# Experts' Silu in one ScalarE function, the attention phase's last jobs in a written-out order, and half of the slot table's one-hots on GpSimd

## The reference, cut to what matters

```
x = x + concat(conv_out, attn_out) @ w_out
h2 = rms_norm(x, norm_ffn_g)
lg, le = h2 @ w_rg, h2 @ w_re            # 4 groups, 32 experts
group = argmax(lg); the two best experts of the group; combine weights
for each block of 128 rows with the same expert e (rows padded per expert):
    y = (silu(xe @ w_g[e]) * (xe @ w_u[e])) @ w_d[e]
    out[token of the row] += y * weight of the row
x = x + out
```

## Time and profile before

| | |
|---|---|
| median of three runs | 2318.94 us |
| the profiled execution, its own time | 2315.55 us |
| its span, first to last instruction | 2313.8 us |
| mean granted TensorE clock | 0.971 |
| PE, DVE, ACT, POOL busy | 93, 73, 57, 33% |

### The profile page before, as it was taken

One profiled execution on the slowest core, in us unless ns is written; L12 is line 12 of the kernel. 1 busy time (PEld: TensorE's weight loads), 2 busy tenths in 40 slices (PEclk: granted clock), 3 DMA queues, 4 the chain that ended last, 5 costly groups with the idle time before them and its releaser, 6 DMA issues. The chain is left out here.

```text
span 2313.8 us, 39978 instructions
## 1 busy us (share of the span) xinstructions
PE 2144.3 (93%) x13278; PEld 1787.7 (77%) x13279; DVE 1687.2 (73%) x2330; ACT 1312.6 (57%) x2435; POOL 755.1 (33%) x678
## 2 busy tenths in 40 slices
PE   8999999994899998899999857999999999999997
PEld 6888888883777886678777745888888888888886
DVE  3798999983676667777888748788688566466644
ACT  5223434334677677766666614678688456465533
POOL 1110565552566554544544501111111111111111
PEclk9999999996999999999999977999999999999999
DMA  6543333325433242332321119999899778768852
GB/s 218 192 157 105 114 124 131 105 100 164 125 94 106 88 132 69 115 116 69 108 79 58 51 73 330 342 311 374 271 374 374 253 215 273 227 220 276 275 173 45
DMA packets 209244, 406.62 MB, mean 176 GB/s; under 512 B 50623, under 2 KB 77119, under 8 KB 209117
## 3 DMA queue, kind: packets, MB, share of 16 engines
q1 hardware_dynamic: 195581, 355.71, 43.8%
q0 software_dynamic: 13536, 49.29, 9.0%
HBM read 312.27 MB, written 92.67 MB: 175 GB/s over the span
## 5 line engine op out<-in xcount | busy, mean ns | idle before, releaser
L2143 DVE TENSOR_TENSOR p_w_lo<-p_raw,p_w_hi 128x1024 fp32r<-128x1024 f32 x384 | 445.9, 1219 | 179.4 <-ACT p_w_hi L1945 175.8
L1790 POOL TENSOR_TENSOR p_wgt<-p_wgt,p_past 128x1024 f32<-128x1024 f32 (+4 forms) x166 | 307.9, 1856 | 354.0 <-DVE p_past L1670 353.8
L1945 ACT ACTIVATE p_w_hi<-p_raw 128x1024 fp32r<-128x1024 f32 x384 | 376.9, 1051 | 62.5 <-PE p_up L2031 51.8
L563 DVE SCALAR_TENSOR_TENSOR p_ut<-p_ut,p_cw 128x512 f32<-128x512 f32 (+1 forms) x480 | 339.5, 782 | 0.0
L1670 DVE TENSOR_TENSOR_SCAN p_past<-p_keep,p_past,p_one 128x513 f32<-128x513 f32 (+1 forms) x196 | 225.9, 1193 | 78.0 <-ACT p_keep L1480 75.4
L298 PE MATMUL p_pj<-p_w_hi,p_xt_hi 128*128 128x512 f32 x680 | 270.9, 398 | 4.2 <-DVE p_xt_lo L539 2.4
L298 PE MATMUL p_pj<-p_w_hi,p_xt_lo 128*128 128x512 f32 x680 | 266.5, 392 | 0.0
L298 PE MATMUL p_pj<-p_w_lo,p_xt_hi 128*128 128x512 f32 x680 | 265.9, 391 | 0.0
L1480 ACT ACTIVATE p_keep<-p_zp 128x512 f32<-128x512 f32 (+3 forms) x326 | 160.2, 547 | 123.1 <-PE p_zp L1351 110.4
L2031 PE MATMUL p_gp<-p_w_lo,p_xt_hi 128*128 128x256 f32 x736 | 206.8, 281 | 0.0
L2031 PE MATMUL p_gp<-p_w_hi,p_xt_lo 128*128 128x256 f32 x736 | 206.7, 281 | 0.0
(11 more groups left out here) (266 smaller groups left out, 4949.0 us busy)
## 6 DMA issues: line engine op xcount, KB each, us to landing
p_raw<-in_w_up SPq DMA_DIRECT2D x128, 512.0 KB
p_raw<-in_w_gate SPq DMA_DIRECT2D x128, 512.0 KB
p_raw<-in_w_down SPq DMA_DIRECT2D x128, 512.0 KB
p_w_raw<-in_w_in SPq DMA_DIRECT2D x40, 256.0 KB, 4.1
p_x<-in_x SPq DMA_DIRECT2D x17, 512.0 KB, 4.3
p_y<-in_x SPq DMA_DIRECT2D x17, 512.0 KB
scr_y<-p_y SPq DMA_DIRECT2D x17, 512.0 KB, 3.0
p_y<-scr_y SPq DMA_DIRECT2D x17, 512.0 KB
```

The costliest lines, as they stand in the source:

```text
L563: dve.scalar_tensor_tensor(dst, src, cw[:, a, j:j + 1], dst, ALU.mult, ALU.add).then_inc(tap_done, 1)
L1790: pool.tensor_tensor(mine, mine, past_rows[:, u % NP, 0:n, 2:2 + w], ALU.mult).then_inc(a_done, 1)
L1945: act.activation(w_hi[:, p, :], raw[:, n % RING, :], ACT.Copy).then_inc(whi_done, 1)
L2143: dve.tensor_tensor(w_lo[:, p, :], raw[:, n % RING, :], w_hi[:, p, :].bitcast(F32), ALU.subtract).then_inc(wlo_done, 1)
```

## The change

In `attention_jobs`, the jobs planned for the steps from the end of the units on are put away, and a list of 14 steps takes their place, with the same jobs. In the tail, `squares` comes in the step of the second `wo` half and `hidden` one step after it (two for the last tile), and DVE's `mean_squares` stands ahead of the jobs. For `o`, ACT squares first and copies second. `rank` no longer uses `le` as scratch.

In `phase_moe`, DVE makes the table of blocks first and then waits for POOL's constants, five instead of six; POOL writes `in_row`. Each half of `gp` gets one Silu by ACT and one multiplication by DVE, without waits of DVE for itself. The second half of transposed `h` gets a place of its own in the unused half of a `gp` bank, PE transposes it before the down projection, and ACT and DVE split it ahead of the next block's rows.

```diff
+    z = 2 * NT - 1
+    tail = [[], [], [("wo", z - 1, 0)], [("h2t", z - 2, 0), ("h2t", z - 2, 1)], [("o", z)],
+            [("wo", z - 1, 1), ("mix", z), ("route", z - 2)], [("wo", z, 0), ("h2t", z - 1, 0), ("h2t", z - 1, 1)],
+            [("wo", z, 1)], [("route", z - 1)], [("h2t", z, 0), ("h2t", z, 1), ("rank", len(BATCHES) - 2)],
+            [("route", z)], [], [], [("rank", len(BATCHES) - 1)]]
...
-        hidden_step = [{m: e + (3 + c if e < len(units) else 2) for m, e in end_step.items() if m >= NT} for c in range(2)]
+        hidden_step = [{m: e + (3 + c if e < end else 1 if m < 2 * NT - 1 else 2)
+                        for m, e in end_step.items() if m >= NT} for c in range(2)]
+        square_step = {m: e + 1 if e < end else e for m, e in end_step.items() if m >= NT}
...
-                    pe.wait_ge(o_sq_done, j[1] + 1)
+                    pe.wait_ge(o_out, j[1] + 1)
...
+                    if i:
+                        act.wait_ge(o_ms, i)
+                    act.activation(o_sq[:, :], rows, ACT.Square).then_inc(o_sq_done, 1)
                     if i >= 2:
                         act.wait_ge(o_done, i - 1)
                     act.activation(o_raw[:, i % 2, :], rows, ACT.Copy).then_inc(o_out, 1)
-                    if i:
-                        act.wait_ge(o_ms, i)
-                    act.activation(o_sq[:, :], rows, ACT.Square).then_inc(o_sq_done, 1)
...
+                elif s - 1 in o_step_of:
+                    mean_squares(o_step_of[s - 1])
...
-        htp = ps("htp", [P, FT, P])
+        htp = ps("htp", [P, 2, P])
+        h_cols = [htp[:, :, :], gp[:, 0, HF:2 * HF].rearrange("p (f t) -> p f t", f=2)]
...
-                act.wait_ge(gs_done[k], b)
-                act.activation(sg[:, bass.ts(k, HF)], gp[:, k, 0:HF], ACT.Sigmoid).then_inc(sg_done[k], 1)
+                act.wait_ge(h_done[k], b)
+                act.activation(sg[:, bass.ts(k, HF)], gp[:, k, 0:HF], ACT.Silu).then_inc(sg_done[k], 1)
...
                 h_hi(b, 0)
+                h_hi(b, 1)
                 x_hi(b + 1)
-                h_hi(b, 1)
...
                     transpose_h(b, 0)
                     transpose_x(b + 1)
+                    transpose_h(b, 1)
                     weights(e, 3)
...
                     half_down(0, 0, True)
-                    transpose_h(b, 1)
                     half_down(1, 0, True)
...
-            dve.wait_ge(consts, 6)
-            link(dve.tensor_copy(iota[:, :], iota_i[:, :]))
...
             dve.sem_inc(table_done, 1)
 
+            dve.wait_ge(consts, 5)
+            link(dve.tensor_copy(iota[:, :], iota_i[:, :]))
...
+            dve.sem_inc(rows_done, 1)
...
-                dve.tensor_scalar(in_row[:, n % RS, :], iota[:, :], row[:, n:n + 1], None, ALU.is_equal)
...
-                dve.tensor_tensor(sg[:, cols], gp[:, k, 0:HF], sg[:, cols], ALU.mult).then_inc(gs_mid[k], 1)
-                dve.wait_ge(gs_mid[k], b + 1)
                 dve.wait_ge(ht_ps[k], b)
                 dve.tensor_tensor(h[:, cols], up[:, cols], sg[:, cols], ALU.mult).then_inc(h_done[k], 1)
-                dve.wait_ge(h_done[k], b + 1)
-                dve.sem_inc(gs_done[k], 1)
...
             def block_of(b, at):
                 rest(at, 0, 1)
-                silu(b, 0)
+                gated(b, 0)
                 rest(at, 1, 2)
+                gated(b, 1)
                 h_rest(b, 0)
-                silu(b, 1)
+                h_rest(b, 1)
                 x_rest(b + 1)
-                h_rest(b, 1)
                 rest(at, 2, PIECES)
...
+            pool.wait_ge(rows_done, 1)
+            for n in range(NC):
+                if n >= RS:
+                    pool.wait_ge(spread, n - RS + 1)
+                pool.tensor_scalar(in_row[:, n % RS, :], iota[:, :], row[:, n:n + 1], None,
+                                   ALU.is_equal).then_inc(row_in, 1)
```

More of the change, by code:

```diff
@@ L903, in attention_jobs @@
         s += 1
+    z = 2 * NT - 1
[3 more added lines that the diff above has]
+            [("route", z)], [], [], [("rank", len(BATCHES) - 1)]]
+    assert sorted(j for x in tail for j in x) == sorted(j for s in placed if s >= end for j in placed[s])
+    placed = {s: js for s, js in placed.items() if s < end} | {end + n: js for n, js in enumerate(tail)}
+    where.update({j: end + n for n, js in enumerate(tail) for j in js})
     return placed, where, first, last, user
@@ L1538, in _ @@
                     decode_mask()
-                for m in at_step(end_step, s - 1):
-                    if m >= NT:
-                        squares(m)
+                for m in at_step(square_step, s):
+                    squares(m)
         @block.vector
@@ L1643, in job @@
                     for k in range(2):
-                        link(dve.tensor_tensor(le[:, 0:hi - lo, :], oh[k][:, 0:hi - lo, :], cand[:, 0:hi - lo, :],
-                                               ALU.mult))
-                        link(dve.tensor_reduce(picks.rank[:, k, lo:hi], le[:, 0:hi - lo, :], AX.X, ALU.add))
+                        mine = oh[k][:, 0:hi - lo, :]
+                        link(dve.tensor_tensor(mine, mine, cand[:, 0:hi - lo, :], ALU.mult))
+                        link(dve.tensor_reduce(picks.rank[:, k, lo:hi], mine, AX.X, ALU.add))
             def piece(n):
@@ L1709, in _ @@
                     second_half(s - 3)
-                if s - 1 in o_step_of:
+                if s < len(units) and s - 1 in o_step_of:
                     mean_squares(o_step_of[s - 1])
@@ L1958, in h_hi @@
                 act.wait_ge(d_done, b)
-                act.activation(ht_hi[:, 2 * k:2 * k + 2, :], htp[:, 2 * k:2 * k + 2, :], ACT.Copy).then_inc(hh_done[k], 1)
+                act.activation(ht_hi[:, 2 * k:2 * k + 2, :], h_cols[k], ACT.Copy).then_inc(hh_done[k], 1)
             def block_of(b, at):
@@ L1964, in block_of @@
                 lead(at, 0, 1)
-                sigmoid(b, 0)
+                gate(b, 0)
                 lead(at, 1, 3)
-                sigmoid(b, 1)
+                gate(b, 1)
                 h_hi(b, 0)
+                h_hi(b, 1)
                 x_hi(b + 1)
-                h_hi(b, 1)
                 lead(at, 3, 6)
@@ L2005, in transpose_h @@
                 pe.wait_ge(h_done[k], b + 1)
-                for f in (2 * k, 2 * k + 1):
-                    last = pe.transpose(htp[:, f, :], h[:, f * P:(f + 1) * P], ident[:, :])
+                for x in range(2):
+                    f = 2 * k + x
+                    last = pe.transpose(h_cols[k][:, x, :], h[:, f * P:(f + 1) * P], ident[:, :])
                 last.then_inc(ht_ps[k], 1)
@@ L2168, in block_of @@
                 rest(at, 0, 1)
[L2169 removed]
+                gated(b, 0)
                 rest(at, 1, 2)
+                gated(b, 1)
                 h_rest(b, 0)
[L2172 removed]
+                h_rest(b, 1)
                 x_rest(b + 1)
[L2174 removed]
                 rest(at, 2, PIECES)
[L2177 removed]
+            for done in (xl_done, *h_done, *hl_done):
                 dve.sem_inc(done, 1)
```

14 lines of the change are left out of this document (7 added, 7 removed).

## The result

The changed kernel takes 2292.8 us (median of four runs, 2290.51 to 2294.42) against 2319.5 us of the kernel before (four runs beside it, 2317.93 to 2320.57): ratio 0.9885, 95% interval 0.9868 to 0.9902. I had forecast 2290 us, range 2279 to 2302. The profiled execution's own time is 2291.98 us, its span 2290.2 us; before they were 2315.55 and 2313.8.

A forecast was written before the change was run, and what follows sets the result against it. A chain through all engines bounds the attention tail, PE the experts' blocks. Terms -15.6 + 0.0 - 4.5 - 8.7 - 0.4 = -29.2 us on 2315.55 give 2286.3, plus the median's 3.4: 2290 us, range 2279 to 2302.

The forecast's parts named there:

- Part 1: Tail of attention: the new order of jobs brings -15.6 us, between -12 and -18.
- half of the 1.8 us that the full clock would give: Tail, Square to router's result: PE idle before this `route` too, so only half the full-clock gain; 15.3 us earlier in all.
- The rival that the picks of batch 3 hold up the last row: Tail: the last row's chain waits for DVE's picks; tail gains only -9 us, 2296 us in all; chance 0.12.
- Part 2: Slot table at the start of the experts' phase: 0.0 us, between -6.1 and +3.
- my 0.55 us a row: Slot table loop: POOL's and DVE's instructions one after the other for the 28 rows not made ahead, 15.4 us.
- the rival, free sharing: Slot table: POOL and DVE don't hold each other up, 6 us more go, 2284 us; chance 0.2.
- the 1.5 us for the block table first: Start of experts' phase: the block table needs no constant, so DVE starts at 1382.3, not 1383.85: -1.5 us.
- Parts 3 and 4: Experts' blocks: 27 intervals without splitting weights gain -4.5 us, 18 with splitting -8.7 us.
- The DMA's rival: Weights' DMA bounds the 12 one-block experts' intervals, staying at 19.26 us; 7.7 us not gained, 2297 us; chance 0.1.
- the splitting blocks' 0.64 us: Blocks with splitting: down projection 0.42 us earlier plus 0.23 us of transposes; -7.7 us over 12 intervals.
- The gain of the first block: First experts' block: adds -0.4 us to the sum.
- the rival of a slower kernel: Experts' blocks: ACT reloads tables at each change between Silu and Copy; 2336 us, or 2349 without the blocks' gain; chance 0.04.

The follow-up runs named there:

- PE kept busy: Kernel with rows shared between POOL and DVE, plus matmuls nobody reads filling PE's idle times: 2282.3 us, ratio 0.9845 to the kernel before.
- Table set once: One single-column Silu by ACT behind the phase's first Exp: 2283.2 us on the changed kernel, 2273.2 us with shared rows and PE kept busy (64 transposes).
- first rows alone: Changed kernel, but DVE stands still until POOL has written its first six one-hot rows: 2295.6 us (single run).

## Why the prediction was right, and where it was not

**Part 1, the tail: right, 1.1 us too much.** Forecast -15.6, measured -14.5. To the end of the last values 6.24 (I took 6.3); then, event by event, `o` came 3.24 us nearer to the values (3.1), `mix` 0.38 to `o` (0.3), the last `wo` 3.61 to `mix` (3.6), the Square 0.95 to `wo` (1.1). The step that failed is the next one, Square to the router's result: I took half of the 1.8 us that the full clock would give, plus 0.3 us for `mean_squares`; the step went from 9.36 to 9.27 us. The `route` stayed at 3.60 us, fully at half clock, and the run with PE kept busy shows what was missing, 7.18 us for this step. The rival that the picks of batch 3 hold up the last row did not come about: DVE's `hidden` started 2.17 us after the Square, at 1353.22, as it had before (2.16). But DVE was busy with picks and copies until that moment, with no time to spare, and nothing in my sum said that it would be just enough: that was luck.

**Part 2, the slot table: the size wrong, +2.6 instead of 0.0.** From DVE's first one-hot to the read it is 19.5 us against 16.5 before, +3.0 where I had +1.1; what lies ahead of that became 0.4 us shorter where I had 1.1. Two terms failed. The first was the price of `in_row` on POOL, 0.29 us from a cast of the same tile, against 0.59 to 0.60 us measured. At 0.59 us, undisturbed, 28 rows are 16.5 us even side by side with DVE (17.2 measured), so the sharing never decided: my 0.55 us a row was near the measured 0.615 for a wrong reason, and the gain of the rival, free sharing, wasn't there to be had. The second was the 1.5 us for the block table first, worth 0.62 alone. The rule of the Trainium skill that I had set beside this (SBUF — State Buffer, "Who interferes with whom") has the right direction: the first row took 1.78 us beside DVE's product of 1088 columns and 0.63 without it. It was not the bound. The range of this part was also added up wrongly: +1.1, +2 and -1.5 make +1.6 at the upper end and not +3, so the measured +2.6 lies outside what my terms allowed.

**Parts 3 and 4, the blocks: right.** Light intervals 18.56 to 18.61 us and once 18.80 (forecast 18.57), one-block 18.57 to 18.62 (18.6), with table loads 20.13 to 20.15 (20.1), in all -13.27 us for -13.2. The DMA's rival is refuted for this kernel: the one-block interval has the same share of 1.05 and 374 GB/s as the earlier trace rows, and still takes 18.57 us. I had put the splitting blocks' 0.64 us down as 0.42 of DVE and 0.23 of the transposes; undone one by one, Silu brings 0.50 and the transposes' place 0.17. The gain of the first block did not show: from the slot table's read to the first `yo` it was 32.38 us before, 32.78 in the changed kernel, and 32.0 to 33.0 in the eight others in which PE wasn't kept busy.

**Table loads.** Eight at the gate's line, as before: Silu and Copy don't drive each other out, and the rival of a slower kernel did not come about. This is what the Trainium skill says of copy (ScalarE: Activation LUTs, "Table sets: the hidden batching unit"), and the trace agrees: 8 loads for 92 Silu. Seven more stand at the line of a Copy (L1958), as before; my prediction did not look at them, and "Table set once" removes them with the eight. I had also taken the gain of parts 3 and 4 off twice in that rival's time: 2289.7 + 59 is 2349 us with the gain, and 2362 without.

**The sum.** The terms give -24.8 us, the profiled executions -23.6, the medians -26.7, against -29.2 forecast: the two misses, tail and slot table, are 3.7 us of the 4.4 between forecast and terms, the first block's 0.8 nearly the rest, and the medians differ by 1.9 us more than the terms, which is within what the unchanged part varies by. So the median's 2292.8 us for 2290 is closer than the terms were: by these it would have been 2294 to 2295. The range's upper end, with part 1 at -12, part 2 at +3 and the DMA's rival, is 2304 us by its own terms and not 2302.

## What to carry to other kernels

Moving an instruction to another engine needs its price there, from the same operation with the same kinds of operands; with a cast's price I halved it. If the price is higher than on the first engine, share the work rather than move it. An edit that shortens PE's stream by putting another engine's work ahead of it paid here only once that engine had been relieved: the same place of the transposes, with its order of ACT's and DVE's work, gains 7 us with Silu and costs 28 us without. And look at what stands at the head of a loop: one instruction before it saved 7.6 us inside.

## What the hardware showed that I had not expected

- POOL compares 128x128 f32 with a value for each partition in 0.59 us, undisturbed (first rows alone); DVE does the same in 0.28 us, with the next instruction 0.20 us behind its start.
- DVE's shift of 128x32, an instruction of 0.18 us, takes 0.98 us beside POOL's memset of 128x1024, in all eleven kernels that have the block table first, and 0.18 us in the kernel before, where the memset had ended.
- PE's granted clock was at half behind an idle time of about 2.2 us in the tail (1.00 until 1355, then 0.50), and again behind 2.5 us at 1380; with the first of these times filled it stayed at 1.00 until 1358, and with the second filled by 64 transposes it was at 1.00 from 1372 on. Half the clock cost 1.65 us on a `route` of 16 matmuls.
- The 15 table loads in the blocks, 1.28 us each, hang on what ran before their loop: behind Exp they are there, behind one Silu of one column there is none.
- The unchanged part before the tail ends up to 8 us apart from one trace to another (1321.8 to 1329.7 us).
